# Two turns of a dense feed forward, each moved into the middle of a matrix product

## The reference

```python
def swiglu(h, w_gate, w_up, w_down):
    return (jax.nn.silu(h @ w_gate) * (h @ w_up)) @ w_down

x = x + jnp.concatenate([out_a, out_b], axis=-1) @ ev_w_out[i]
h = rms_norm(x, ev_ffn_norm[i])
x = x + swiglu(h, ev_w_gate[i], ev_w_up[i], ev_w_down[i])      # (256,1024) @ (1024,2816), ... @ (2816,1024)
# layer 1
x = x + mixer_c(rms_norm(x, od_attn_norm[i]), ...)
x = x + moe_swiglu(rms_norm(x, od_ffn_norm[i]), ...)           # 8 experts, width 3584
```

## Time and profile before

| | |
|---|---|
| median of 3 runs | 1410.12 us (1409.87 to 1410.13) |
| profiled execution, own time | 1411.29 us |
| its span | 1409.1 us |
| PE busy | 1374.0 us, 98% of the span |
| DVE busy | 1155.0 us, 82% |
| ACT busy | 1043.0 us, 74% |
| mean granted PE clock | 0.992 |
| memory traffic | 429.01 MB, mean 304 GB/s |

### The profile page before, as it was taken

How to read it: one execution, slowest core, us unless ns; L and a number is a source line. 1 busy time by engine, 2 the same in 40 slices (tenths; PEclk the granted TensorE clock), 3 DMA queues, 4 the chain that set the end, 5 groups by cost and what they waited for, 6 DMA issues and landing times.

```text
span 1409.1 us, 19439 instructions
## 1 busy us (share of the span) xinstructions
PE 1374.0 (98%) x6501; PEld 1129.3 (80%) x6501; DVE 1155.0 (82%) x1450; ACT 1043.0 (74%) x1350; POOL 134.2 (10%) x204
## 2 busy tenths in 40 slices
PE   9989999999899999999999999999999999999997
PEld 7757788888677888888888888888888888888885
DVE  4856555456987999889899899989889998998996
ACT  5667444447886888878878887887887888788786
POOL 0400000000712810000000000000000000000000
PEclk9989999999999999999999999999999999999999
DMA  9706854304628999999999999999999999999980
GB/s 327 277 1 228 308 181 139 110 1 145 259 77 313 384 387 369 384 376 388 366 373 389 377 391 373 373 386 370 401 353 388 385 366 386 378 383 370 372 329 15
DMA packets 132066, 429.01 MB, mean 304 GB/s; under 512 B 4225, under 2 KB 11564, under 8 KB 132028
## 3 DMA queue, kind: packets, MB, share of 16 engines
q1 hardware_dynamic: 129232, 418.50, 78.9%
q0 software_dynamic: 2480, 8.95, 2.5%
q10 hardware_dynamic: 316, 1.07, 0.2%
HBM read 422.21 MB, written 6.29 MB: 304 GB/s over the span
## 4 chain that ended last, share of the span: by engine, by line
PE 83%; issue 6%; DVE 5%; ACT 3%; DMA 2%; SPq 1%; POOL 0%; DVEq 0%; POOLq 0%; ACTq 0%
PE bank L753 26%; PE bank L755 26%; PE bank L754 26%; PE bank L713 2%; DMA ring<-in_ev_w_in_dram 1%; DVE w_lo L1670 1%; ACT w_hi L1173 1%; DMA out_dram<-h,idx_t 0%; PE bank L675 0%; SPq L521 0%; PE bank L899 0%; PE bank L964 0%; DVE ring L1763 0%; DVE mx L1882 0%; DMA ring<-in_od_w_ukv_dram 0%
## 5 line engine op out<-in xcount | busy, mean ns | idle before, releaser
L1598 DVE TENSOR_TENSOR w_lo<-ring,w_hi 128x1024 fp32r<-128x1024 f32 x544 | 644.0, 1220 | 34.9 <-ACT w_hi L1105 21.2
L1105 ACT ACTIVATE w_hi<-ring 128x1024 fp32r<-128x1024 f32 x544 | 571.1, 1062 | 129.7 <-PE bank L755 129.7
L753 PE MATMUL bank<-w_hi,hT_hi 128*128 128x512 f32 (+3 forms) x1088 | 418.2, 384 | 1.3 <-DVE hT_lo L1690 0.7
L755 PE MATMUL bank<-w_lo,hT_hi 128*128 128x512 f32 (+3 forms) x1088 | 416.2, 383 | 0.0
L754 PE MATMUL bank<-w_hi,hT_lo 128*128 128x512 f32 (+3 forms) x1088 | 415.8, 382 | 0.0
L753 PEld LDWEIGHTS bank<-w_hi,hT_hi 128*128 128x128 f32 x1088 | 204.4, 188 | 42.6 <-issue 3.2
L755 PEld LDWEIGHTS bank<-w_lo,hT_hi 128*128 128x128 f32 x1088 | 204.4, 188 | 39.6
L754 PEld LDWEIGHTS bank<-w_hi,hT_lo 128*128 128x128 f32 x1088 | 204.5, 188 | 39.0
L1670 DVE TENSOR_TENSOR w_lo<-ring,w_hi 128x1024 fp32r<-128x1024 f32 (+3 forms) x124 | 140.3, 1142 | 97.6 <-ACT w_hi L1173 97.5
L753 PE MATMUL bank<-w_hi,aT_hi 128*128 128x512 f32 x490 | 194.7, 397 | 3.3 <-issue 1.9
L755 PE MATMUL bank<-w_lo,aT_hi 128*128 128x512 f32 x490 | 191.4, 391 | 0.0
(11 more groups left out here) (335 smaller groups left out, 1185.0 us busy)
## 6 DMA issues: line engine op xcount, KB each, us to landing
ring<-in_od_e_gate_dram SPq DMA_DIRECT2D x57, 2048.0 KB, 10.0
ring<-in_od_e_up_dram SPq DMA_DIRECT2D x56, 2048.0 KB, 10.1
ring<-in_od_e_down_dram SPq DMA_DIRECT2D x56, 2048.0 KB, 10.3
ring<-in_ev_w_gate_dram SPq DMA_DIRECT2D x5, 2048.0 KB, 9.2
ring<-in_ev_w_up_dram SPq DMA_DIRECT2D x5, 2048.0 KB, 9.9
ring<-in_ev_w_down_dram SPq DMA_DIRECT2D x5, 2048.0 KB, 7.8
ring<-in_ev_w_in_dram SPq DMA_DIRECT2D x8, 512.0 KB, 9.5
ring<-in_ev_w_in_dram SPq DMA_DIRECT2D x2, 2048.0 KB, 15.8
```

Of the source, the lines that this page charges most:

```text
L753: pe.matmul(dst, hi, whi, start=first, stop=False)
L755: return pe.matmul(dst, hi, wlo, start=False, stop=final)
L1105: act.activation(e_hi_at[place_of(q)], eights(ring[:, i % RING, j * QUARTER:(j + 1) * QUARTER]), ACT.Copy).then_inc(hi_ready, 1)
L1598: dve.tensor_tensor(e_lo_at[place_of(q)], eights(ring[:, i % RING, j * QUARTER:(j + 1) * QUARTER]), e_hi_at[place_of(q)].bitcast(F32), ALU ...
```

## The change

The first turn moves into the gate product of chunk 1, behind its second quarter. For that, gate 1 is computed into banks 6 and 7 in place of 2 and 3, and it no longer waits for DVE to have read up 0 out of banks 2 and 3. Banks 6 and 7 are used by down 0 next, so PE waits there for the Silu of chunk 1. The last turn moves into the down product of chunk 4, behind its second quarter. Its two parts go into `hT_hi` and `hT_lo`, as the normed input is no longer read by then, and the down product of chunk 5 reads them there. The functions on ACT and DVE follow the same order.

```diff
         def gate_bank(c):
 
-            return 2 * (c % 2) if c else 4
+            return (4, 6)[c] if c < 2 else 2 * (c % 2)
+
+        LAST_CHUNK = (D_FF - 1) // NW
+
+        def turns_after(p, q):
+
+            if q != p["q0"] + 1:
+                return None
+            return 0 if p["kind"] == "gate" and p["c"] == 1 else \
+                LAST_CHUNK if p["kind"] == "down" and p["c"] == LAST_CHUNK - 1 else None
+
+        def hidden_at(c):
+
+            return (aT_hi, aT_lo) if c < LAST_CHUNK else (hT_hi, hT_lo)
...
-                    if p["kind"] == "gate" and c >= 1:
+                    if p["kind"] == "gate" and c >= 2:
                         pe.wait_ge(hidden_ready, c)
                     if p["kind"] == "up" and c >= 1:
                         pe.wait_ge(aT_lo_ready, c)
                     if p["kind"] == "down":
-                        if c == chunks - 1:
-                            turn(c)
+                        if c == 0:
+                            pe.wait_ge(silu_ready, 2)
                         pe.wait_ge(aT_lo_ready, c + 1)
                     base = {"gate": gate_bank(c), "up": 2 - 2 * (c % 2), "down": 4}[p["kind"]]
                     for q in range(p["q0"], p["q1"]):
                         if p["kind"] == "down":
-                            product(q, lambda t, half: bank[4 + 2 * t + half], sT(aT_hi), sT(aT_lo))
+                            hi, lo = hidden_at(c)
+                            product(q, lambda t, half: bank[4 + 2 * t + half], sT(hi), sT(lo))
                         else:
                             product(q, lambda t, half: bank[base + t], sT(hT_hi), sT(hT_lo))
-                    if p["kind"] == "up" and c == 0 or p["kind"] == "down" and c < chunks - 2:
-                        turn(c if p["kind"] == "up" else c + 1)
+                        if turns_after(p, q) is not None:
+                            turn(turns_after(p, q))
+                    if p["kind"] == "down" and c < chunks - 2:
+                        turn(c + 1)
...
-                    if p["kind"] == "down" and p["q1"] == pieces[stage_pieces("ffn")[-1]]["q1"]:
-                        turned(c)
                     for q in range(p["q0"], p["q1"]):
                         split_to(q + LEAD)
+                        if turns_after(p, q) is not None:
+                            turned(turns_after(p, q))
...
-                    if p["kind"] == "up" and c == 0 or p["kind"] == "down" and c < ffn_chunks - 2:
-                        turned(c if p["kind"] == "up" else c + 1)
+                    if p["kind"] == "down" and c < ffn_chunks - 2:
+                        turned(c + 1)
...
-                    o = act.activation(aT_hi[:, 2 * m:2 * m + 2, :].rearrange("p a n -> p (a n)"),
+                    o = act.activation(hi[:, 2 * m:2 * m + 2, :].rearrange("p a n -> p (a n)"),
                                        bank[2 * (c % 2) + m][:, :], ACT.Copy)
```

More of the change, by code:

```diff
@@ L1906, in turned @@
                     two = lambda b: b[:, 2 * m:2 * m + 2, :].rearrange("p a n -> p (a n)")
-                    o = dve.tensor_tensor(two(aT_lo), bank[2 * (c % 2) + m][:, :], two(aT_hi).bitcast(F32),
+                    o = dve.tensor_tensor(two(lo), bank[2 * (c % 2) + m][:, :], two(hi).bitcast(F32),
                                           ALU.subtract)
@@ L1914, in ffn @@
                     c = p["c"]
-                    if p["kind"] == "down" and n == stage_pieces("ffn")[-1]:
-                        turned(c)
                     for q in range(p["q0"], p["q1"]):
                         split_to(q + LEAD)
+                        if turns_after(p, q) is not None:
+                            turned(turns_after(p, q))
                     if p["kind"] == "up":
```

## The result

The changed kernel takes 1406.26 us (median of 13 runs, 1405.37 to 1408.53) against 1409.87 us for the kernel before on the same chip (13 runs, 1408.25 to 1410.99). The ratio is 0.9975, with a 95% interval of 0.9967 to 0.9983: 3.6 us faster, between 2.4 and 4.7. The same kernel was timed once more later, beside other runs of before: 0.9973 (0.9963 to 0.9984).

The account below looks back on a forecast made before the run. The prediction took PE to set the pace, idle at two turns waiting for DVE. Gains of 1.71 + 1.64 = 3.35 us off a median of 1410.12 gave 1406.8 us, range 1405.8 to 1408.8 us.

Parts of the forecast that it names:

- PE sets the pace and its idle time is worth its length: Dense feed forward: ACT and DVE run ahead of PE, so each microsecond of PE standing still is lost.
- Site 1: Turn of chunk 0, between up 0 and gate 1: 3.05 us against 1.34 undisturbed, a gain of 1.71 us.
- Site 2: Turn of chunk 5, between down 4 and down 5: 2.58 us against 0.94 undisturbed, a gain of 1.64 us.
- The leads: After the moved turns, ACT and DVE finish before PE needs them: 2.8 us at up 1, 4 us at down 5.
- The copy in ACT's queue: ACT's copy of chunk 0 starts up 1's second-quarter split 1.9 us late, still leaving 4.3 us of lead.
- The gain lasts: Behind the feed forward everything hangs on PE's progress, so the shift passes whole; clock allowance 0.7 us either way.
- the prediction's own signs: Wrong if PE newly waits over 0.3 us at up 1, down 0 or down 5, or down-5-to-end changes over half a microsecond.
- The sum and the median: Whole kernel: 1.71 + 1.64 = 3.35 us gained, median 1410.12 - 3.35 = 1406.8 us.
- One site only: Rival: a wait returns, most likely at up 1, so only one site pays; 1408.4 us, chance 0.09.
- Given back later: Rival: layer-1 mixer or first expert meets a transfer or clock limit, losing the gain; 1409.6 us, chance 0.08.
- The clock falling at a turn inside a product: Rival: granted clock falls behind the turn in gate 1 and down 4; slower, 1414 us, chance 0.04.
- A wait still in the queue: Rival: a remaining wait, such as for `lo_ready`, holds gate 1 at 148.8 us; 1410.1 us, chance 0.03.

Follow-up runs that it names:

- The run with one quarter less: Both turns behind the third quarter of their product, against the changed kernel's second; dense stage 188.50 us, profile only.
- the one with two less: Changed kernel with the turn of chunk 0 behind the last quarter of gate 1; dense stage 192.83 us, ratio to before 1.0004.
- the two halves: Two kernels, each moving only one turn against the kernel before: chunk 0 alone, ratio 0.9985; chunk 5 alone, ratio 0.9984.
- the filled kernel: Changed kernel plus 3 plain float32 matmuls in PE's idle ahead of the layer-0 attention turn for heads 8 and 9; median 1405.66 us, ratio to before 0.9969.

## Why the prediction was right

- *PE sets the pace and its idle time is worth its length.* Shown: 15 matmuls more cost 3.42 us of the stage, and 3.42 = 191.86 - 188.44.
- *Site 1, 1.71 us.* Measured 1.69 alone (191.82 - 190.13). Counting from start to start was right: the recorded idle of 1.50 would have been 0.2 short. It begins only at the recorded end of the last matmul, 0.39 us after its start, where the next one usually starts after 0.227.
- *Site 2, 1.64 us.* Measured 1.67 alone. The undisturbed turn of four transposes took 0.90 us and not my 0.94.
- *The leads.* 2.8 us at up 1: in the rows of the changed kernel below, ACT copies from 153.86, DVE is done at 154.98 + 1.29 = 156.27, and up 1 begins at 159.11. The run with one quarter less had 0.1 us of lead and no wait, the one with two less waited 2.5 us. One statement was off: ACT's idle ahead of its first copy is 2.48 us and not "about 2 us or less".
- *The copy in ACT's queue.* The split behind it had its buffer free at about 152.95 and began at 154.83, 1.9 us late as predicted. It was low at 156.19 + 1.22 = 157.41, with PE wanting it 4 us later; a lead shrank and the sum stayed. The Trainium skill's page "PSUM — Partial Sum Buffer", section "Engine vs sequencer instructions", states that the queues of ScalarE, VectorE and GpSimdE are strictly first in, first out. The trace agrees: the split began behind the copy and not ahead of it.

```profile
153.86 1.09 ACT L1398 ACTIVATE aT_hi<-bank 128x512 fp32r<-128x512 f32 x2 [2.48 <-PE bank L977]
154.83 1.06 ACT L1189 ACTIVATE w_hi<-ring 128x1024 fp32r<-128x1024 f32 x1
154.98 1.29 DVE L1925 TENSOR_TENSOR aT_lo<-bank,aT_hi 128x512 fp32r<-128x512 f32 x2 [2.35 <-ACT aT_hi L1398]
156.19 1.22 DVE L1687 TENSOR_TENSOR w_lo<-ring,w_hi 128x1024 fp32r<-128x1024 f32 x1
159.11 0.39 PE L766 MATMUL bank<-w_hi,hT_hi 128*128 128x512 f32 x1
```

- *The gain lasts.* Shown by the parts behind the stage, and for 3.4 us in the other direction; the mixer and the experts took the same time in every profile within 0.7 and 0.4 us. Of the prediction's own signs, one was crossed by a hair. From the start of the last matmul of down 5 to the end it is 1093.7 us before, and 1093.1 and 1093.2 after, 0.6 and 0.5 shorter, where more than half a microsecond was to mean an error. It is no loss, and the other profiles lie between 1093.0 and 1093.6; where it comes from is not shown. The experts started 5.3 us earlier in the first profile after and not 3.3, as the front was 1.5 and the mixer 0.4 us shorter too.
- *The sum and the median.* 3.35 us predicted, 3.38 in the stage, 3.6 (2.4 to 4.7) by the timed runs. The median of 1406.26 lies 0.5 below the 1406.8 predicted. Half of that is the starting point: the prediction took 1410.12 from three runs, and 13 runs of before gave 1409.87. The other half is well inside the interval, so that the close hit of the median is partly luck, and that of the stage is not.
- *Rivals.* One site only: ruled out by the two halves. Given back later: ruled out by the lengths of the parts behind the stage, of the changed kernel and of the one with extra work. The clock falling at a turn inside a product: ruled out, it was 1.00 there in every run. A fall of the clock did come in the dense stage, but where PE stood still for 2.5 us at the end of a product, and not where it worked. A wait still in the queue: ruled out, none is left at either site.

The forecast of the median rests on a difference alone, 1410.12 - 3.35. The offset of 1.17 us between the profiled execution and the median is added and taken away again, so nothing here tests it. The two profiled executions differ by 5.5 us, and a comparison of them alone would have missed by 2.

## What to carry to other kernels

When one engine sets the pace and hands work to others that it needs back, put the hand-over into the middle of its next long piece of work, with at least the round trip of the others behind it: here one quarter of product, 2.7 us, hid the copies, none left a wait of 2.5 us, and more than one brought nothing. Price a wait from start to start against the same passage undisturbed, and look at the clock behind it if the wait is long. To prove a gain of a quarter per cent, cut the profile at fixed instructions and compare the parts: the part with the change repeated within 0.1 us, while whole executions scattered by 2 to 3.

## What the runs showed of the hardware

- An idle of 1.5 us ahead of eight transposes, or of 1.4 us behind four, left the granted clock at 1.00 in every profile with one (before and the two with one site). 2.5 us of idle behind eight transposes was followed by 0.61 over 4.4 us, with the matmuls 0.43 us apart, and 11 matmuls in its place kept 1.00. In the attention, an idle of 3.0 us had a fall of the clock beside it in all ten profiles that have that idle (0.77 to 0.88 over the 13 to 15 us behind it), and none in the one where three matmuls filled it (1.00). These lengths are too few to say where the border lies.
- The front scattered by 3.4 us between identical programs of that part, and mostly with the clock: 121.75 us at a mean of 0.94 from 70 to 100 us, 122.68 to 123.78 at 0.89, 123.92 to 124.92 at 0.83 and 0.84, 125.14 at 0.79. It matters where the clock falls: the filled kernel, also at 0.94, had 123.08, since its fall was in 96 to 100 us and not in 76 to 80. A part without a fall was the shortest of its kind in both places, 13.16 and 32.87 us.
- At a granted clock of 1.00, a matmul of 512 columns with plain float32 operands was two instructions of 0.44 us each (20 in 8.75 us), where one of the fast kind takes 0.227 us from start to start: nearly four times as much.
